# Three output tiles in every entry, and squares summed by column groups, in a 1-core chain of transformer sublayers

## The reference, cut to what matters

```python
def second_block(x, ...):
    h = x
    for i in range(DEPTH_2):                       # 2 layers
        f = swiglu(rmsnorm(h, g[0]), ffn_gate[i, 0], ffn_up[i, 0], ffn_down[i, 0])
        h = h + MACARON * rmsnorm(f, g[1])
        mix = hybrid_mixer(rmsnorm(h, g[2]), ...)
        h = h + rmsnorm(mix, g[3])
        f = swiglu(rmsnorm(h, g[4]), ffn_gate[i, 1], ffn_up[i, 1], ffn_down[i, 1])
        h = h + MACARON * rmsnorm(f, g[5])
        gate = jax.nn.sigmoid(rmsnorm(h, g[6]) @ w_ple_gate[i])
        h = h + rmsnorm((p[i] @ w_ple[i]) * gate, g[7])
    return h
```

## Time and profile before

| | |
|---|---|
| median of 3 runs | 3004.22 us (3003.27 to 3006.89) |
| the profiled execution | 3005.28 us, its span 3003.5 us |
| PE busy | 2862.1 us, 95% of the span |
| DVE, ACT, POOL busy | 1558.5, 1145.5, 243.3 us |
| mean granted clock of TensorE | 0.980 |

### The profile page before, as it was taken

One profiled execution on the slowest core, in us unless ns is written; L12 is line 12 of the kernel. 1 busy time (PEld: TensorE's weight loads), 2 busy tenths in 40 slices (PEclk: granted clock), 3 DMA queues, 4 the chain that ended last, 5 costly groups with the idle time before them and its releaser, 6 DMA issues.

```text
span 3003.5 us, 42576 instructions
## 1 busy us (share of the span) xinstructions
PE 2862.1 (95%) x17236; PEld 2384.8 (79%) x17236; DVE 1558.5 (52%) x2618; ACT 1145.5 (38%) x1861; POOL 243.3 (8%) x272
## 2 busy tenths in 40 slices
PE   6999889899999999999999999899999999999997
PEld 3866888778788888777888888788888778888886
DVE  5744465544354434855644436644436755644346
ACT  3333444243333323455433224532324564333234
POOL 0000065400000000200000000000000201000000
PEclk7999999999999999999999999999999999999998
DMA  6222000022232332301222332233332301332321
GB/s 237 64 67 73 3 8 3 15 91 92 77 106 98 98 106 92 117 32 50 72 97 98 99 106 78 77 98 99 98 105 96 95 29 43 98 98 93 104 91 57
DMA packets 69778, 244.92 MB, mean 82 GB/s; under 512 B 8464, under 2 KB 10640, under 8 KB 68944
## 3 DMA queue, kind: packets, MB, share of 16 engines
q1 hardware_dynamic: 69584, 242.21, 24.5%
HBM read 234.70 MB, written 3.15 MB: 79 GB/s over the span
## 4 chain that ended last, share of the span: by engine, by line
PE 67%; DVE 3%; ACT 2%; issue 1%; DVEq 0%; ACTq 0%
PE pair L228 20%; PE pair L230 20%; PE pair L229 20%; PE pair L2568 2%; PE pair L2597 2%; PE pair L357 2%; PE pair L2607 1%; ACT w_hi_at L182 1%; DVE rstd_at L473 1%; DVE work_at L308 0%; DVE w_lo_at L190 0%; PE pair L491 0%; DVE residual L314 0%; DVE h_lo_at L319 0%; PE pair L488 0%
## 5 line engine op out<-in xcount | busy, mean ns | idle before, releaser
L228 PE MATMUL pair<-h_hi_at,w_hi_at 128*128 128x512 f32 (+1 forms) x2048 | 781.3, 381 | 35.9 <-DVE h_lo_at L319 31.4
L229 PE MATMUL pair<-h_lo_at,w_hi_at 128*128 128x512 f32 (+1 forms) x2048 | 759.1, 371 | 0.0
L230 PE MATMUL pair<-h_hi_at,w_lo_at 128*128 128x512 f32 (+1 forms) x2048 | 759.0, 371 | 0.0
L190 DVE TENSOR_TENSOR w_lo_at<-w_raw,w_hi_at 128x1024 fp32r<-128x1024 f32 x348 | 439.4, 1263 | 430.6 <-ACT w_hi_at L182 430.4
L182 ACT ACTIVATE w_hi_at<-w_raw 128x1024 fp32r<-128x1024 f32 x348 | 364.8, 1052 | 523.5 <-PE pair L230 512.1
L228 PEld LDWEIGHTS pair<-h_hi_at,w_hi_at 128*128 128x128 f32 x2048 | 389.0, 190 | 112.2 <-DVE h_lo_at L319 37.4
L229 PEld LDWEIGHTS pair<-h_lo_at,w_hi_at 128*128 128x128 f32 x2048 | 389.1, 190 | 67.1 <-issue 0.5
L230 PEld LDWEIGHTS pair<-h_hi_at,w_lo_at 128*128 128x128 f32 x2048 | 388.9, 190 | 65.3
L2330 DVE TENSOR_TENSOR work_at<-pair,rstd_at 128x512 f32<-128x512 f32 (+1 forms) x184 | 122.1, 667 | 363.2 <-PE pair L230 363.1
L228 PE MATMUL pair<-a_hi_at,w_hi_at 128*128 128x512 f32 (+1 forms) x792 | 290.1, 366 | 0.0
L229 PE MATMUL pair<-a_lo_at,w_hi_at 128*128 128x512 f32 (+1 forms) x792 | 289.4, 365 | 0.0
(11 more groups left out here) (423 smaller groups left out, 3975.8 us busy)
## 6 DMA issues: line engine op xcount, KB each, us to landing
w_raw<-in_weights SPq DMA_DIRECT2D x431, 512.0 KB, 3.4
residual<-in_x SPq DMA_DIRECT2D x1, 2048.0 KB, 12.0
cos_sin_at<-rope_table SPq DMA_DIRECT2D x2, 1024.0 KB, 4.8
by_sin_at<-delta_at SPq DMA_DIRECT2D x32, 64.0 KB, 2.0
by_sin_at<-kd_at SPq DMA_DIRECT2D x32, 64.0 KB, 2.0
out<-residual SPq DMA_DIRECT2D x16, 128.0 KB, 1.7
q_wide<-in_ctx SPq DMA_DIRECT2D x1, 1024.0 KB, 12.9
rope_table<-zb SPq DMA_DIRECT2D x1, 1024.0 KB, 4.2
```

Source lines behind the costliest of these rows:

```text
L190: eng.tensor_tensor(self.w_lo[:, g % self.split].rearrange("p k n -> p (k n)"), self.w_raw[:, g % RAW], self.w_hi[:, g % self.split].rearr ...
L228: pe.matmul(out, sh, mh, start=start, stop=False)
L229: pe.matmul(out, sh, ml, start=False, stop=False)
L230: return pe.matmul(out, sl, mh, start=False, stop=stop)
```

## The change

1. **Entry.** Three output tiles are made for each n; the third runs three n behind (`BEHIND`), in Ple eight. The squares are summed in four batches, at n=4, 8, 12 and behind n=15. A batch is four matmuls with 32 columns of ones, each into its own 32 partitions, hence on its own column group of the array; ACT copies the 128 partial rows (`act_partial`) and one full matmul adds them (`pe_fold`), for half 0 behind n=10 and for half 1 inside tile 3. ACT's squares go one tile later than its rounding.
2. **Granules.** `w_make_hi(g0+2)` goes from ACT's tile 4 to tile 2, `w_make_hi(g0+3)` is added at tile 4; DVE makes the low part of g0+2 at step 3 and of g0+3 at step 8. In all bodies the granule made at t is g0+t+4 where it was g0+t+3. The granule g0+4 stands between the entry's two reciprocals on DVE.
3. **Banks.** The Ffn's gate and up tiles turn over three pairs of banks; the Mixer's twelve tiles have a bank each from a list; in the Mixer's last two tiles both half-0 results share bank 6 and both squares wait for the second. `Exit.pe_sum(0)` of the Mixer stands in tile 6's half 1 (k=2), not in tile 7's (k=1).
4. **First block.** Score matmuls of windowed attention take two key blocks at once (256 columns) where they took one: 2 or 3 matmuls for an item, where there were 4 or 5, over 32 items.

```diff
-            for t in range(KD):
-                self.pe_products(pe, half, t)
-                if self.leave and half == 0 and t == 1:
-                    self.leave.pe_sum(pe, 1)
-                if t >= 1:
-                    self.pe_sum(pe, half, t - 1)
-            self.pe_sum(pe, half, KD - 1)
+        for n in range(2 * KD):
+            if n in (4, 8, 12):
+                self.pe_sums(pe, n // 4 - 1)
+            for m in range(2):
+                self.pe_product(pe, n, m)
+            if self.leave and n == 1:
+                self.leave.pe_sum(pe, 1)
+            if n >= self.BEHIND:
+                self.pe_product(pe, n - self.BEHIND, 2)
+            if n == 10:
+                self.pe_fold(pe, 0)
+        self.pe_sums(pe, 3)
+        for n in range(2 * KD - self.BEHIND, 2 * KD):
+            self.pe_product(pe, n, 2)
...
+    def pe_sums(self, pe, batch):
+
+        half, second = divmod(batch, 2)
+        pe.wait_ge(*self.squared(4 * batch + 4))
+        for q in range(4):
+            last = pe.matmul(self.kit.banks[self.SUM_BANK[half]][32 * q:32 * q + 32, 0:HALF], self.kit.square("ones")[:, 0:32],
+                             self.sq[:, q], start=not second, stop=bool(second), skip_group_check=True)
+        last.then_inc(self.summed.sem, 1)
...
-                    if half == 1 and t == KD - 1 and k == 1:
+                    if half == 1 and t == KD - 2 and k == 2:
                         self.exit.pe_sum(pe, 0)
...
         for t in range(self.TILES):
-            kit.w_make_hi(act, g0 + t + 3)
+            if t < self.TILES - 1:
+                kit.w_make_hi(act, g0 + t + 4)
...
+                if half == 0 and t == 2:
+                    kit.w_make_hi(act, self.g0 + 2)
                 if half == 0 and t == 3 and leave:
                     leave.act_squares(act, 1)
                 if half == 0 and t == 4:
                     if leave:
                         leave.act_root(act, 1)
-                    kit.w_make_hi(act, self.g0 + 2)
+                    kit.w_make_hi(act, self.g0 + 3)
...
-        makes = {KD: lambda: kit.w_make_lo(dve, self.g0 + 2)}
+        makes = {3: lambda: kit.w_make_lo(dve, self.g0 + 2), KD: lambda: kit.w_make_lo(dve, self.g0 + 3)}
```

More of the change, by code:

```diff
@@ L348, in dve_rstd @@
[L348 to L370, removed]
@@ new lines, in pe_fold, with pe_product @@
+    def pe_fold(self, pe, half):
+        pe.wait_ge(*self.part_copied(half + 1))
+        pe.matmul(self.kit.banks[self.SUM_BANK[half]][:, HALF:], self.kit.square("ones"), self.partial[:, cols(half)],
+                  start=True, stop=True).then_inc(self.folded.sem, 1)
+    def pe_product(self, pe, n, m):
+        kit, (half, t) = self.kit, divmod(n, KD)
+        c = cols(half)
+        if m == 0:
+            pe.wait_ge(*self.h_ready(n + 1))
+        if n == 0:
+            pe.wait_ge(kit.w_split, self.g0 + m + 1)
+        last = matmul3(pe, kit.banks[self.FIRST_BANKS[m]][:, c], kit.w_tile(self.g0 + m, t),
+                       (self.hi[:, t, c], self.lo[:, t, c]), t == 0, t == KD - 1)
+        if n == 2 * KD - 1:
+            last.then_inc(kit.w_used, 1)
@@ L2840, in dve @@
                    b["kd"][:, t - 8])
-            for bank, c in self.entry.first_parts(t) if t < 2 else [(self.bank(t), slice(0, SEQ))]:
-                last = dve.tensor_tensor(dst[:, c], bank, kit.rstd[:, c], ALU.mult)
-            last.then_inc(self.drained.sem, 1)
+            dve.tensor_tensor(dst, self.bank(t), kit.rstd[:, :], ALU.mult).then_inc(self.drained.sem, 1)
+            if 0 < t < self.TILES - 1:
+                kit.w_make_lo(dve, g0 + t + 4)
         for r in (6, 7):
@@ L2990, in pe @@
                 self.before.exit.pe_sum(pe, 1)
[L2991 to L2994 removed]
+            if t == 5:
+                self.entry.pe_sums(pe, 0)
         pe.wait_ge(*self.emb_drained(KD))
[L2997 to L3008 removed]
+        for n in range(2 * KD):
+            for m in range(2):
+                self.entry.pe_product(pe, n, m)
+            if n >= KD:
+                self.entry.pe_product(pe, n - KD, 2)
+            if n == 0:
+                self.entry.pe_sums(pe, 1)
+            if n == KD + 2:
+                self.entry.pe_fold(pe, 0)
+            if n == KD + 4:
+                self.entry.pe_sums(pe, 2)
+        self.entry.pe_sums(pe, 3)
+        for n in range(KD, 2 * KD):
+            self.entry.pe_product(pe, n, 2)
+        for t in range(3, self.full):
             if t >= 4:
@@ L3014, in pe @@
                                k == KD - 1)
+                if t == 3 and k == 0:
+                    self.entry.pe_fold(pe, 1)
             last.then_inc(kit.w_used, 1)
```

184 lines of the change are left out of this document (100 added, 84 removed).

## The result

The changed kernel takes 3016.16 us (median of 16 runs, 3009.85 to 3019.61), the kernel before 3005.62 (16 runs, 3002.56 to 3008.63). The ratio is 1.0032, 95% interval 1.0025 to 1.0039: slower by 10.5 us. The forecast was 3003.4 with a range to 3013, so both the sign and the range were missed. The profiled execution took 3013.12 us, span 3011.3; against the span before it is +7.85, which is 2.7 less than the medians differ.

What follows compares the result with a forecast made beforehand. PE, busy 95%, was taken as the bound outside the entries, where it waits on the residual chain to h_lo. Terms summed to -6.8 us (clock holds) or +5.3 (falls); the middle, -0.8, gave a median of 3003.4, range 2988 to 3013.

Steps and rivals of the forecast that it cites:

- The sums: Eight entries: batches at 0.76 us each cut an entry's sums from 6.9 to 3.9 us, 24 us in all.
- rival D: In 32 batches, the column groups run one after another: 0.96 us more each, +31 us, 3034; chance 0.03.
- What the third tile changes: Mixer's entry, n=4 to tile 3: third tile may fill PE's waits; 20.8 us becomes 18.5 plus 0.43, 1.9 shorter.
- What it delays: Entries behind an exit: DVE's low part of g0+2 at step 3 makes n=1 2.4 us and h_lo(4) 1.5 later.
- The second column: Whole kernel: sum if the clock falls behind new idle times, +5.3 us, against -6.8 if it holds.
- The Mixer's tile 6: Both Mixers, ahead of tile 6: PE waits 2.6 us for roots behind granule g0+9; +5.2, or +8.6 if clock falls.
- Ple's entries: Ple's two entries: third-tile products after the last h and ACT's later fifth square cost +0.3 us each, clock holding.
- The clock: Behind new idle times of 2.4 to 2.7 us: a fall costs 1.2 to 1.7; middle of both sums, -0.8, taken.
- Rival C: Entries: clock falls behind each new gap between n=0 and n=1, batches at n=4 slower; about +9 us, 3013; chance 0.15.
- Windowed attention: First block: paired score matmuls save at most 3.2 us over 32 items; -2.0 taken as DVE and ACT share the period.
- Rival A: PE-bound entries: all 24 us of sums and most of 31.4 us of waits go; about -45, 2959; chance 0.12.
- B: Entries: the granule at step 3 is harmless, the 1.5 us is lost in none of six; -9, 2994; chance 0.15.

Runs made afterwards that it cites:

- the second experiment: Changed kernel with granule g0+2's high part moved behind the exit's squares on ACT and its low part to DVE's step 6: 2996.92 us, ratio 0.9967.
- its mended form: Changed kernel with the Mixer's two roots ahead of granule g0+9 and granule g0+2 moved behind the exit's squares: 2992.67 us, ratio 0.9960.

## Why the prediction was wrong, by its own steps

**The sums: right in price.** 0.76 for a batch was measured as 0.76. Taking the column groups away cost 30.5 by the medians, rival D's 31, but 25.0 between the profiled executions: the forecast put all 32 batches on the path, and the first of an entry lies in a wait. (1.14 - 6 x 0.12 is 0.42, not 0.43; it changes nothing.)

**What the third tile changes: right.** From n=4 to tile 3 was forecast 18.5, 2.3 less, of which the second fold in tile 3 takes 0.43 back; 18.65 was measured, 2.2 less. With both granules moved, this leaves the Mixer's entry 1.0 shorter up to L2511 and an Ffn 2 to 3.

**What it delays: right in mechanism and place, too small in price.** n=1 was forecast 2.4 late and idled 2.51. h_lo(4) was forecast 1.5 late; with the clock held by useless matmuls it was 1.6 late, and in the changed kernel's Mixers 2.3 and 3.1, as the exit's second sum then runs at the lower clock. The second column has 1.15 for such an entry; layer 0, with a fall of 3.4 us, measured 1.2, and layer 1, with one of 6.8, measured 2.0. Moving the granule saved some 3 in each of the five entries behind an exit. In the Ffn behind Ple, where I let the earlier root outweigh it, PE idled 3.83 behind n=0 and stayed at the lower clock for the 13 us shown above: +0.2 for a forecast -1.7 to -0.5.

```profile
1900.60 0.58 PE L228 MATMUL pair<-h_hi_at,w_hi_at 128*128 128x256 f32 x1 [3.83 <-DVE h_lo_at L323]
```

**The Mixer's tile 6: right.** An idle time of 2.6 was forecast and 2.41 measured; the place cost 2.7 without a fall and 4.3 with one (the second column's 4.3).

**The Mixer's exit: right.** A gain of 2.4 and an idle time of 0.9 were forecast; alone it gave 2.5 and 0.79 in each place, and 0.79 in the changed kernel too.

**Ple's entries: wrong, the term that was mis-sized most.** I said +0.3 each. The batches make PE's list in the embedding 2.4 shorter, but the drains on ACT end when they did, so PE idles 2.67 where it idled 0.25, and with 1.59 more behind that the clock falls for 7 us (in the kernel before, for 3.4 us behind 1.58 in layer 0 and not at all in layer 1). Work saved ahead of a wait saves nothing; what I left out is that it costs, once it becomes idle time. Measured +0.7 and +3.8. With matmuls put into it, they are -0.2 and +1.3.

```profile
1834.09 0.39 PE L228 MATMUL pair<-h_hi_at,w_hi_at 128*128 128x256 f32 x1 [2.67 <-ACT emb_at L3073]
...
1836.30 0.58 PE L228 MATMUL pair<-h_hi_at,w_hi_at 128*128 128x256 f32 x1 [1.59 <-DVE w_lo_at L190]
```

**The clock: the step that failed.** I had both columns, knew of a fall behind 3.31 and none behind 1.62, and then took the middle of the columns, -0.8. Each of the new idle times of 2.4 to 2.7 brought a fall in this profile, so the second column, +5.3, was the case, and +7.85 was measured. Rival C was nearest to the 3016.16. Its 3013 is added up wrongly: 5.3 + 2 + 3 is 10.3 and not 9, and 3004.22 + 10.3 is 3014.5; the range's end, which is C's 3013, was 1.5 too low by its own terms. The price was low too: I had 3 to 4 us at the lower clock for each fall, and several lasted 7 and one 13. Why some last longer was not tested. The columns are two states, and their mean is the forecast of neither; as 11 of 14 idle times of 2.4 to 2.5 brought a fall, the second should have had most of the weight.

**Windowed attention: wrong.** -2.0 was forecast, some two thirds of the 3.2 that PE saves at most, and 0.4 came at equal clock, so I gave PE far too large a share of an item's period; what has the rest was not tested. That the table's first block is at -2.5 is luck.

Rival A (all of the sums and most of the waits go) was refuted by the result, and B by DVE's wait of 1.13 at step 3. What B describes is what the second experiment made true by moving the granule, and it was worth 15 to 19 for its 9.

What stays open: the changed kernel's median is 3 above its profiled run. Its seven slowest runs (3017.4 to 3019.6) have a mean granted clock of 0.975 or 0.976 and the nine others 0.976 to 0.980, so more time at the lower clock goes with them; where it lies in them was not seen. Nor was it found why the same idle time brings a fall in one execution and none in another.

## What to carry to other kernels

When a weight's split or any other bookkeeping moves one step ahead in a list, look at what stands behind it in that list: each of the two granules here waited for something that came just too late, and both cost next to nothing elsewhere (behind the roots; in DVE's own wait). Work taken off the bounding engine ahead of a wait becomes idle time, and here an idle time of 2.41 us on TensorE cost 1.6 more wherever a fall followed it; price such gaps at the worse state, not at the mean. Two parts of a change may each be worth little without the other, so undo them one by one before judging them. And before a difference of 1 us between two executions is put down to an edit, look whether the clock was the same in both: in windowed attention 0.9 of 1.3 was the clock.

## What the hardware showed that was not expected

Useless matmuls in idle time saved 12.3 us in the changed kernel and 7.1 in its mended form (8.5 and 4.1 by the stretches of the profiled executions), and nothing that could be told in the kernel before nor at idle times of 1.6 to 1.9. The lower clock lasted about 3.4, 7 and 13 us at a time in the windows above, and 13 of these were a stretch in which PE was busy for 7.05 us only. Four matmuls on 32 columns each, as a batch between full matmuls, cost 0.76 us: 0.57 from the batch's start to the next product's, and 0.1 each in front of it and behind that product's start. By the Trainium skill, "TensorE: Matmul & The Clock Gate", Part 3, weight loads overlap running matmuls only where the row group differs; here it is one row group, and the eight records still took 0.64 us and not the 1.7 of the full ones, so whatever doesn't overlap there is small in this case.
